# Output product in early and late halves over the heads, up sums by tile, down loads reordered: one core of a Trainium2 chip

## What is computed

```
h = rmsnorm(x) * g;  q, k, v of 8 "fox" heads and 8 "sb" heads = h @ w_in
o = concat(rmsnorm(fox_attention) * fox_g, rmsnorm(stick_breaking_attention) * sb_g)
x = x + o @ w_out                                    # the output product
h = rmsnorm(x) * ffn_g
gate, val = split(causal_dwconv(h @ w_up))           # the up products, 2 x 2816 columns
x = x + (silu(gate) * val) @ w_down                  # the down products
return rmsnorm(x) * final_g
```

## Time and profile before

| | us |
|---|---|
| median of 3 runs (lowest, highest) | 2593.56 (2593.15, 2594.3) |
| the profiled execution, its own time | 2595.39 |
| its span, first to last instruction | 2593.6 |
| TensorE busy | 2504.9 (97%) |
| VectorE busy | 1503.9 (58%) |
| GpSimd busy | 1094.3 (42%) |
| ScalarE busy | 1025.9 (40%) |
| mean granted clock of TensorE | 0.992 |

### The profile page before, as it was taken

One profiled execution on the slowest core, in us unless ns is written; L12 is line 12 of the kernel. 1 busy time (PEld: TensorE's weight loads), 2 busy tenths in 40 slices (PEclk: granted clock), 3 DMA queues, 4 the chain that ended last, 5 costly groups with the idle time before them and its releaser, 6 DMA issues. The chain is left out here.

```text
span 2593.6 us, 31686 instructions
## 1 busy us (share of the span) xinstructions
PE 2504.9 (97%) x12594; PEld 2087.6 (80%) x12594; DVE 1503.9 (58%) x1450; ACT 1025.9 (40%) x1517; POOL 1094.3 (42%) x630
## 2 busy tenths in 40 slices
PE   8999999999999999999999999999979999988999
PEld 4888788888888888888788888887758888877887
DVE  5864557665666853445635455465876767664324
ACT  3421144434254430024556566564344444441214
POOL 3754443433343345542120211134567787852320
PEclk9999999999999999999999999999989999999999
DMA  8222221212121153242110110132212222234411
GB/s 340 82 88 71 103 86 57 74 54 66 62 81 62 56 194 133 89 156 72 34 41 34 41 41 33 41 114 82 93 45 73 98 74 92 79 122 171 146 41 65
DMA packets 65214, 226.07 MB, mean 87 GB/s; under 512 B 7816, under 2 KB 11784, under 8 KB 63792
## 3 DMA queue, kind: packets, MB, share of 16 engines
q1 hardware_dynamic: 48800, 169.00, 18.5%
q10 hardware_dynamic: 16272, 55.09, 6.0%
HBM read 174.22 MB, written 45.65 MB: 85 GB/s over the span
## 5 line engine op out<-in xcount | busy, mean ns | idle before, releaser
L264 POOL TENSOR_TENSOR w_hi<-w_raw,ones 128x1024 fp32r<-128x1024 f32 x73 | 193.5, 2651 | 580.3 <-PE G L238 471.7
L238 PE MATMUL G<-H_hi,w_hi 128*128 128x512 f32 x928 | 290.1, 394 | 1.0 <-ACT silu_zB L724 0.7
L269 POOL TENSOR_TENSOR w_lo<-w_raw,w_hi 128x1024 fp32r<-128x1024 f32 x88 | 240.8, 2736 | 114.6 <-ACT w_hi L263 109.0
L238 PE MATMUL G<-H_lo,w_hi 128*128 128x512 f32 x928 | 286.0, 389 | 0.0
L238 PE MATMUL G<-H_hi,w_lo 128*128 128x512 f32 x928 | 285.8, 389 | 0.0
L238 PEld LDWEIGHTS G<-H_lo,w_hi 128*128 128x128 f32 x928 | 174.2, 188 | 36.5
L238 PEld LDWEIGHTS G<-H_hi,w_lo 128*128 128x128 f32 x928 | 174.2, 188 | 36.5
L238 PEld LDWEIGHTS G<-H_hi,w_hi 128*128 128x128 f32 x928 | 171.6, 188 | 36.9 <-issue 3.7
L1952 POOL TENSOR_TENSOR w_lo<-w_raw,w_hi 128x1024 fp32r<-128x1024 f32 x24 | 60.2, 2507 | 319.9 <-ACT w_hi L2176 319.9
L2065 PEld LDWEIGHTS G<-att_v,probsT 128*128 128x128 f32 x1152 | 146.6, 192 | 22.2 <-ACT probsT L2205 13.8
L2007 PE MATMUL G<-A_hi,w_hi 128*128 128x512 f32 x368 | 152.5, 414 | 8.9 <-DVE projected L2377 8.4
(11 more groups left out here) (577 smaller groups left out, 6265.8 us busy)
## 6 DMA issues: line engine op xcount, KB each, us to landing
w_raw<-w_in SPq DMA_DIRECT2D x65, 512.0 KB, 3.3
up_raw<-w_up SPq DMA_DIRECT2D x44, 512.0 KB, 5.0
pre_raw<-w_in SPq DMA_DIRECT2D x30, 512.0 KB, 3.3
act_d<-made SPq DMA_DIRECT2D x22, 512.0 KB, 2.9
wm<-w_mod SPq DMA_DIRECT2D x8, 1024.0 KB, 18.5
w_raw<-w_out SPq DMA_DIRECT2D x16, 512.0 KB, 3.3
x_d<-x ACTq DMA_DIRECT2D x16, 512.0 KB, 2.7
x<-x_d SPq DMA_DIRECT2D x16, 512.0 KB, 7.7
```

What stands on the lines that cost most here:

```text
L238: mm = nc.tensor.matmul(dst[:, n * NB:n * NB + c], w[:, k, :], m[:, k, n * NB:n * NB + c], start=first, stop=last)
L264: eng.tensor_tensor(dst, src, ones.unsqueeze(1).to_broadcast([P, kt, P]), ALU.mult)
L269: nc.gpsimd.tensor_tensor(w_lo[:, slot, 0:kt, :], w_raw[:, slot, 0:kt, :], w_hi[:, slot, 0:kt, :].bitcast(F32), ALU.subtract).then_inc(w_r ...
```

## The change

1. *Attention's end.* The tiles are loaded in the order 4, 5, 6, 7, 0, 1, 2; the fox tiles go to a place of their own (`fox`) and are no longer split by GpSimd there. VectorE waits for `x` at step 120 and norms tiles 0 to 3 at steps 121, 123, 125 and 127. The sb heads' root, reciprocal and diagonals are made at steps 126 and 127.
2. *The output product.* TensorE makes all eight early halves and then all eight late halves, in the order 0, 2, 4, 6, 1, 3, 5, 7 of the output tiles. A weight part (`load_parts`) holds either the sb rows or the fox rows of two slabs. The fox heads are multiplied with their norm first (`fox normed`, VectorE), then split (`fox hi` ScalarE, `fox lo` GpSimd), so a late half is added to `X2` as it is. Results rotate over three pairs of banks. Weight high parts from part 2 on are made by ScalarE, not by GpSimd.
3. *The up sums.* VectorE makes the sums of pairs of tiles as soon as these are scaled, between the late halves; one of the four is GpSimd's. Pass 0 runs its products in the order 11, S1, S4, 12, S2, S3, 22; S2 and S3 wait for the last quarter of their sums alone. The squares are summed into eight columns, with the root at 128x8, then spread through diagonals.
4. *The down loads.* In SP's order: weights 0 and 1 once the pass before the last is split; tiles 0 to 7 when product 12 of the last pass ends; the stores of the last two activations; weights 2, `x3` tiles 0 and 1, weights 3; then tiles 8 to 13 and `x3` 2 to 7 in turns. `x3` has a semaphore for each tile. VectorE splits tiles 0 to 3 and 5 to 7, among its work of the last pass, GpSimd only tile 4.

```diff
-        EARLY_TILES = [4, 5, 6, 0, 1, 2, 7]
+        HEAD_TILES = [4, 5, 6, 7, 0, 1, 2]
+        OUT_ORDER = (0, 2, 4, 6, 1, 3, 5, 7)
+        EARLY_PAIRS = [(G[1], G[0], U2)[k % 3] for k in range(KT)]
+        LATE_PAIRS = [(U2, G[1], G[0])[i % 3] for i in range(KT - 2)] + [G[1], U2]
...
-            for k in EARLY_TILES:
+            for k in HEAD_TILES:
                 sp.wait_ge(o_stored[k], 16)
-                sp.dma_start(A[1][:, k, :].bitcast(F32), o_d[k]).then_inc(o_landed[k], 16)
+                sp.dma_start(A[1][:, k, :].bitcast(F32) if k >= HEADS else fox[:, k, :], o_d[k]).then_inc(o_landed[k], 16)
...
-            for k in range(1, KT):
+            for k in range(2, KT):
                 early(k)
-                S.wait(pe, "dve", "out2 late", k - 1)
-                late(k, range(HEADS), True, True).then_inc(gemm_done, 1)
+            for i in range(KT):
+                late(i)
...
+            parts_high(HEADS)
+            parts_high(HEADS + 1)
+            for i, k in enumerate(OUT_ORDER):
+                if i in (2, 4):
+                    parts_high(HEADS + i // 2 + 1)
+                if i == 6:
+                    for name in ("11", "S4", "12"):
                         slab_high(act, 0, name)
+                    S.wait(act, "dve", "sums 1 to 0")
+                    S.mark("act", "sums' high part 1", act.activation(T_hi[:, 2, 0:1], T_raw[:, 2, 0:1], ACT.Copy), 0)
+                if i == 7:
+                    for name in ("S1", "S2"):
+                        slab_high(act, 0, name)
+                if i:
+                    scaled_high(OUT_ORDER[i - 1])
...
-                if s == STEPS - 2:
-                    v.wait_ge(x2_landed, 16 * KT)
-                    normed(0)
-                    normed(1)
+                if s == STEPS - TT:
+                    v.wait_ge(x2_landed, 16 * KT)
+                if s >= STEPS - TT and s % 2:
+                    normed((s - STEPS + TT) // 2)
...
+            for i, k in enumerate(OUT_ORDER):
+                if i:
+                    out2_low(OUT_ORDER[i - 1])
                 me("out2 with sb", k)
...
+                late_made(v, i)
+                if i < KT - 1:
+                    do("out2 job", v.tensor_tensor(X2[:, k, :], X2[:, k, :], LATE_PAIRS[i], ALU.add), k)
...
+                if 1 <= i <= 4:
+                    first_sums(i - 1)
+                if i in (5, 6):
+                    second_sums(i - 5)
+                if i == 6:
+                    S.wait(v, "act", "sums' high part 0")
+                    me("sums 1 to 1")
+                    do("sums' low part 0", v.tensor_tensor(T_lo[:, 3], T_raw[:, 3], T_hi[:, 3].bitcast(F32), ALU.subtract))
...
-        POOLED_TILES = 4
+        POOLED_TILES = (4,)
...
+            S.wait(sp, "pool", "low 22", END_P - 1)
+            load_down(0)
+            load_down(1)
+            S.wait(sp, "pe", "product 12", END_P)
+            for t in range(6):
+                load_tile(t)
...
+            store_act(END_P - 1)
...
+            store_act(END_P)
+            load_down(2)
+            load_x3(0)
+            load_x3(1)
+            load_down(3)
...
+            gate_second(END_P)
+            value_second(END_P)
+            for t in (1, 2, 3):
                 tile_low(t)
+            conv(END_P, 0)
+            value_first(END_P)
             conv(END_P, 1)
+            for t in range(5, KT):
+                tile_low(t)
             product_made(END_P)
```

More of the change, by code:

```diff
@@ L2580, in load_up @@
                 else:
-                    S.wait(sp, "dve", "out2 last late 0")
+                    S.wait(sp, "dve", "out2 with sb", KT - 1)
                 for m in range(2):
@@ L2705, in product @@
                 S.mark("pe", f"product {name}", mm, p)
-            for p in range(FT):
+            S.wait(pe, "dve", "out2 lo", KT - 2)
+            S.wait(pe, "dve", "out2 job", 5)
+            product(0, "11")
+            S.wait(pe, "dve", "sums' low part 0")
+            product(0, "S1")
+            S.wait(pe, "dve", "out2 last lo 1")
+            product(0, "S4")
+            S.wait(pe, "dve", "out2 sum", KT - 1)
+            for t in range(TT):
+                mm = pe.matmul(S2[:, t:t + 1], bs[:, 0, t * P:(t + 1) * P], ones[:, 0:1], start=True, stop=True)
@@ new lines, in _ @@
+            S.mark("pe", "out2 summed", mm)
+            S.wait(pe, "dve", "out2 last lo 0")
+            S.wait(pe, "act", "first product", 0)
+            product(0, "12")
+            S.wait(pe, "dve", "sums' low part 1 1")
+            product(0, "S2", ("dve", "sums' low part 1 3"))
+            S.wait(pe, "act", "out2 root")
+            S.wait(pe, "dve", "out2 diagonals")
+            S.mark("pe", "out2 spread", over_features(halves_of(S2), bs[:, 0, :]))
+            S.wait(pe, "pool", "sums' low part 2 0")
@@ L2959, in gate_first @@
+            S.wait(v, "act", "sums' high part 3")
+            do("sums' low part 3", v.tensor_tensor(T_lo[:, 1], T_raw[:, 1], T_hi[:, 1].bitcast(F32), ALU.subtract))
             def gate_first(p):
```

404 lines of the change are left out of this document (240 added, 164 removed).

## The result

The changed kernel takes 2602.39 us (median; 2601.46 to 2604.49), the kernel before, timed beside it, 2594.51: a ratio of 1.0028, 95% interval 1.0017 to 1.0039. It is slower by 0.3%, where the prediction said 0.5% faster and 2590 us at most. The profiled execution has a span of 2601.3 us at a mean granted clock of 0.987, against 2593.6 and 0.992.

The account below looks back on a forecast made before the run. TensorE was busy for 2504.9 of 2593.6 us, so only 88.7 us could be won. Terms +2.3, -3.3 and -12.4 made -13.4: 2582.0 us for the profiled execution, 2580.2 us as median, range 2566 to 2590.

Parts of the forecast that it names:

- Part 4: Seam to the down products: -12.4 us (-17 to -5), with one 6.8 us stop before tile 5 in job 0.
- 1.6 of slow clock: Down job 0: 1.6 us of slow clock, added to the 6.8 us stop before tile 5.
- Part 1: Attention's end: VectorE waits for `x`, loaded behind three more tiles; +2.3 us (0 to +5).
- Part 2, the early halves: Output product, first eight halves: three VectorE instructions of 1.22 us, 3.7 us for 5.43 us of TensorE; no gap.
- stretch A: Output product's start to product 12 of the second up pass: 147.1 us, some 31 of it waiting and slow clock.
- Part 2, the late halves: Output product, last eight halves: additions every 6.35 us (even) or 7.3 (odd) against 5.43; store beside up loads +3.1.
- the light chain: Rival, chance 0.20: late additions keep up, no S4 wait, no contention; product 11 starts at 1869; 2568 us.
- Part 3, behind product 11: Seam to the up products: product 12 of pass 1 at 1920.6 against 1923.9, so -3.3 us (-15 to +5).
- I add 1.3 before tile 5's addition and 2.3 behind it: Seam to the up products: 3.6 us for what engines take from each other, between 0 and some 20.
- Slower, 2600 us: Rival, chance 0.06: full mutual exclusion of VectorE and GpSimd between 1864 and 1900, 22 us in place of 2.5.
- No change: Rival, chance 0.08: stores ahead of the scaling take 6.0 us at five of seven late tiles; 2594 us.
- The down gap is only moved: Rival, chance 0.18: down job 0 stalls 14 us instead of 6.8, -5 in place of -12.4; 2588 us.

Follow-up runs that it names:

- e1: The kernel before with part 4 of the change alone (down loads and split of the tiles): 2588.61 us, ratio 0.9961.
- e2: The changed kernel with part 4 undone, so parts 1 to 3 alone: 2613.56 us, ratio 1.0058.
- e3: The changed kernel with VectorE's early halves keeping operands in PSUM, without the copy of the spread to SBUF: 2598.90 us, ratio 1.0006.
- e4: The changed kernel with VectorE's addition of a late half ahead of the previous tile's low part: 2594.89 us, ratio 0.9986.
- e5: The changed kernel with the third sums and their low parts moved from GpSimd to VectorE: 2596.17 us, ratio 1.0000.
- e7: e4 with ScalarE's square and VectorE's sum of a tile ahead of the scaling of the tile before: 2593.51 us, ratio 0.9991.
- e11: Changed kernel with e3, e4, e5, e6's edits and earlier splits of down tiles 5-7, plus square first and tile 3 scaled before weights S4/12: 2580.53 us, ratio 0.9942.
- e12: Changed kernel with e3, e4, e5, e6's edits, earlier splits of down tiles 5-7, u2 before fourth low part, value half before gate convolution: 2586.30 us, ratio 0.9957.
- e6: The changed kernel with the eight loads of `x` ahead of the last four head tiles in SP's queue: 2600.82 us, ratio 1.0015.

## Why the prediction was wrong

**Part 4: right, a little smaller.** Predicted one stop of 6.8 us before tile 5 and none before job 2; it was 7.1 us there, and no other. Predicted -12.4 us; the tail gave 9.8, 10.2 (e1) and 11.1 (e2). Of the 2.2 us that e1 misses, 0.8 are the term "1.6 of slow clock" (the 12 matmuls behind the stop take 0.43 us each instead of 0.23, 2.4 us) and 0.3 the longer stop; the rest isn't placed. In the changed kernel the tail also begins with the slow clock behind product 12, 2.9 us against 1.8 in the kernel before (1923.90 to 1944.00: 81 matmuls in 20.1 us).

**Part 1: right in its cause, and in its size as far as it can be told.** The wait for `x` came where it was expected; the last `x` landed at 1763.6, which less the 2.6 us by which that trace runs late is 1761.0, against 1761.4 in the prediction. +2.3 us predicted, some 2 us by the means of the last rounds, with a spread as large, and 0 to 2.8 us of TensorE's wait for `att_out`.

**Part 2, the early halves: wrong.** The step that failed is "three VectorE instructions of 1.22 us, 3.7 us for 5.43 us of TensorE ... I see no gap here". They were priced by low parts made when GpSimd had nothing to read. The kernel before had the right price in the same place, one instruction further on, in VectorE's addition beside GpSimd's high part of the weights:

```profile
1807.54 2.18 DVE L2498 TENSOR_TENSOR x<-x,tiles_made 128x1024 f32<-128x1024 f32 x1
...
1806.17 2.46 POOL L264 TENSOR_TENSOR w_hi<-w_raw,ones 128x1024 fp32r<-128x1024 f32 x1 [9.26 <-PE G L2129]
```

It ends at 1809.72, 1.1 us behind GpSimd's 1808.63, and the same meeting comes four times more, every 11 us (2.18 to 2.21 us). In the changed kernel GpSimd splits the fox heads and weights in these very 50 us, and each `fox normed` but the first takes 3.4 us, four `out2 with sb` 2.2 to 3.2. The first addition should have ended 55.8 us behind attention's mark and did so 60.6 us behind it: 4.8 us, of which e3 gave back 3.9, and 3.7 at the end of stretch A.

**Part 2, the late halves: the mechanism right, the period too short.** A period of 6.35 us against 5.43 was predicted; the four up to tile 1 took 6.31, 7.18, 6.30 and 7.73. In each of the two long ones a sum of VectorE's stands behind the low part of weights on GpSimd: 2.79 us at 1849.82 and 2.75 at 1863.30, for 0.68 of its own. That is the exclusion again, where the text had no term for it. The store of tile 1 beside the up loads: 6 us predicted, 6.7 from issue to landing measured (7.7 in e4). Product 11 was to start 103.9 us behind the mark and started 110.9 behind it: 4.8 of the 7.0 us come from the early halves, 2.2 from the period. That TensorE isn't held until product 11 was wrong through the same lag (5.2 us at 1868.52). What this order costs was foreseen too: the light chain had product 11 at 1869 against 1878.9, 9.9 us earlier. In e4 it comes 11.8 us earlier behind the mark, and 9.0 of that are left at product 12. I took it for a property of the change; it was one queue position.

**Part 3, behind product 11: wrong.** From product 11 to product 12 of the second pass it was to be 41.7 us and was 50.3. The step that failed is "I add 1.3 before tile 5's addition and 2.3 behind it". The 1.77 us of the earlier trace rows was read as the price of a meeting. GpSimd's timeline in the kernel before has beside it

```profile
1869.46 2.27 POOL L2647 TENSOR_TENSOR up_sum_S<-up_raw,up_sum 128x512 f32<-128x512 f32 x1
```

which ends at 1871.73, and VectorE's ends 0.54 us later, at 1872.27: it was the rest of one short instruction of GpSimd's, whole. Beside one of 128x1536 the price is 3.3 us (4.49 and 4.52 for 1.22). e5 took back 3.2 us of the 8.6 in this stretch and 2.7 in the tail.

The changed kernel's trace shows where the rest can lie, though no run separates it. VectorE stands idle for less than 0.5 us in all between 1892.5 and 1919; ScalarE's high parts wait for its sums, GpSimd waits for those, and product 12 comes 16.8 us behind GpSimd's first sum (16.5 in the prediction). So what stretches VectorE's instructions there goes straight through. Five are longer than their own time beside GpSimd's, by 1.1 us (1893.64), 0.9 (1895.53), 3.3 (1898.63), 1.1 (1905.84) and 3.3 (1911.07), and two of GpSimd's behind them by 0.9 (1917.97) and 2.1 (1921.33): 12.7 us, where the text had put in 2.3. That is more than the 8.6 us that are missing, so its sum without meetings wasn't exact either, and by how much stays open. The slow clock behind product 11 (0.43 us a matmul) isn't needed for it.

**The rivals.** "Slower, 2600 us", by whole instruction exclusion, has the time (2602) and the mechanism, at a chance of 0.06. That the time agrees is in part luck: its price was counted for one stretch by number of instructions, 22 us, where 12.7 us of stretching are found behind product 11, and 7.0 us of the delay arise ahead of it (4.8 and 2.2), mostly outside that stretch. "No change" didn't come: of the late tiles' stores only tile 1's took much more than 2.6 us to land. "The down gap is only moved" didn't either: the stop was 7.1 us, not 14. The Trainium skill (SBUF — State Buffer, Who interferes with whom) states that a VectorE instruction with two SBUF inputs and a GpSimd one that reads SBUF contend for a shared port pair, that the second to issue is blocked until the first has finished, and that a VectorE instruction with at most one SBUF input, outside its 2-port modes, does not contend. The traces agree on all three points: 1803.14 ends 1.08 us after GpSimd's, GpSimd's of 1896.52 waits for VectorE's, and e3's 1.21 us with one input in PSUM is untouched. The text had weighed that rule and taken a milder one from a single row. That rival also takes 2.5 us out of the sum where 3.6 had been put in; with 3.6 it would be 2598.6.

**Sum.** Predicted +2.3, -3.3, -12.4. Measured by the two traces' lengths: stretch A +12.3 and tail -9.8, and the stretch to attention's end +5.3, of which 2.6 are there before the last round begins, where both run the same code. As the term for A was off by 15.6 us (4.8, 2.2 and 8.6), the sign turned. In its own sum 16.9 us (18.9 less 2.0) behind 1897.4 is 1914.3 and not 1913.9, which changes nothing. Of the 7.9 us between the medians, A and tail are 2.5 and part 1 about 2; the other 3 or so no run assigns.

## What to carry to other kernels

List, for each stretch where work is moved, what GpSimd reads from SBUF in it, and price every VectorE instruction with two SBUF inputs there at its own time plus up to a whole instruction of GpSimd's; with one input left in PSUM it took its own time here. A row that came out longer in an old trace shows the rest of one particular instruction of the other engine, not the price of a meeting. Where stages are pipelined by hand, put the operation that frees the next stage ahead of the tail of the stage before, on every engine of the chain; and when that helps, look first at what the engine with the longest chain (here GpSimd's sums) allows, since further reorderings then win nothing (e7, e11, e12).

## What the runs showed of the hardware

The exclusion holds both ways and for whole instructions, also of 128x1536 (4.5 us for one of 1.2 us; 5.53 for GpSimd's). When the wait ahead of product 12 fell from 4.6 to 1.0 us, the matmuls behind it ran at a granted clock of 1.00 instead of 0.64, which was worth 2.9 us. The length of a gap alone doesn't tell: of four waits of 3.10 us ahead of the same product two were followed by a first matmul of 0.77 us (the changed kernel, e2) and two by one of 0.47 (e3, e6), and in e7 product 11 began at 0.47 behind 4.54 us. A store of 512 KB that was scaled 2.6 us after its issue took 6.8 us beside the up loads (6.7 to its landing). And the same code took between 1740.6 and 1746.0 us up to the same point, a spread as large as most of the effects measured here; only lengths inside a trace, and medians of many runs, told them apart.
